# Token-major residual, output, feed-forward and down projections, and norms taken one 128-token tile at a time

## The chip, the core and the metric

The kernel runs on one core of one Trainium2 chip. The metric is the device time of one execution in microseconds (us), lower is better. An execution is one launch of the whole program, both layers included.

## What is computed

The program computes a decoder trunk of two layers for 256 tokens and a model width of 1024, in float32:

```python
for l in range(2):
    sh1, sc1, g1, sh2, sc2, g2 = split(silu(c) @ ada_w[l] + ada_b[l], 6)      # six vectors of 1024
    h = rmsnorm(x, norm_mix_w[l]) * (1 + sc1) + sh1
    x = x + g1 * hybrid_mixer(h, ...)      # ends in merged @ w_o
    h = rmsnorm(x, norm_ffn_w[l]) * (1 + sc2) + sh2
    ffn = swiglu(h, w1, w3, w2) if l == 0 else moe_swiglu(h, ...)   # dense 2816 wide; top 2 of 8 experts
    x = x + g2 * ffn
return rmsnorm(x, final_norm_w)
```

The mixer projects h to nine groups of 512 columns (f, q, ab, ac, ah, i, v, u, g) and to three gates of 1024. It runs a short convolution, a gated linear recurrence (nine levels of masked scores) and a spatial gating unit (from u and v, called sgu), projects each of the three results to 1024 columns, adds them under their gates to `merged` and multiplies by `w_o`.

## The kernel before

**Precision.** Every weight piece of 128 x 1024 floats is loaded by a DMA into a ring of 11 slots (`raw`) and split into a rounded high part, by ScalarE, and the low rest, by VectorE, in a ring of 6 slots (`split`). The activations are split in the same way (`hS[:, 0]` and `hS[:, 1]`). A product is three matmuls: high by high, high by low and low by high. So a piece costs one DMA, one ScalarE copy (line 1254), one VectorE subtraction (lines 1507 and 2046) and its matmuls, and all the matmuls are issued by one helper (line 671).

**Two shapes of matmul.** Feature-major (`tile`, `project`, `down`): 128 x 128 weights stand still and 256 tokens move, so a piece takes 24 matmuls of 256 columns. The result has features on the partitions. Token-major (`project_rows`, `half_rows`): 128 tokens stand still and 512 weight columns move, so a piece takes 12 matmuls of 512 columns for the two tiles of 128 tokens. In the kernel before, the groups i and v, the gates and the branch projections are token-major. The residual `xT`, `w_o` (8 pieces per layer), the dense `ffn_w1` and `ffn_w3` (44 pieces) and `ffn_w2` (22 pieces) are feature-major. The experts multiply 128 gathered rows at a time, with 6 matmuls of 512 columns per piece.

**Norms.** `norm` on ScalarE and VectorE works on all 256 tokens at once. ScalarE squares `xT`, TensorE sums the squares over the features by a matmul with ones (`stat_sum`, `stat_pair`), ScalarE takes the root, VectorE the reciprocal, then eight chunks of 128 features are scaled, shifted and split. TensorE meanwhile sums the modulation vectors over the partitions (`ada_sum`: 16 instructions of one column) and, before the feed-forward part, runs filler matmuls (`stream`, 12 instructions).

**Order.** All is written out by hand. Each engine runs its own list. `unit_plan` and `event_plan` list which PSUM banks are used in which order and who empties them; `high_parts` and `low_parts` say up to which piece ScalarE and VectorE split before their next step; `dense_pieces` gives the order in which SyncE issues the DMAs, and the next DMA into a slot waits until its piece is used up. The sums behind the modulation vectors are products on VectorE (`product`, lines 1585 and 1588), set among the pieces by lists such as `FFN_TAKE` and `DOWN_TAKE`.

**Levels of the recurrence.** `level(l, j)` on TensorE stands between projection units. VectorE prepares its operands (`prepare(l, j)`) and merges its scores from PSUM (`keep_scores(l, j)`, line 1777, and line 1773 for the last). Levels alternate between two pairs of banks, so TensorE's event n + 2 waits until event n is emptied; after level 8 comes `sgu_mix`, which uses the banks of level 7. In both layers the levels 0 to 8 follow the units ab0, ab1, ac0, ac1, ah0, ah1, i0, v0 and v1.

**From layer 1's w_o to the experts.** After `w_o` and the norm the kernel turns `xT` and the normed rows from feature-major to token-major (32 transposes, line 1068), computes router logits, picks the experts, ranks the tokens and gathers the first 128 rows (`gather`), and the first expert's matmuls begin.

Of the kernel before, what the change touches and what calls it, by code (L numbers as in the profile page):

```python
# [51 lines left out]
WO_ORDER = [(0, 0), (1, 0), (0, 1), (1, 1), (2, 0), (2, 1), (3, 0), (3, 1)]  # L52
# [25 lines left out]
ADA_ORDER = [0, 1, 2, 3, 4, 5, 6, 7, 11, 8, 9, 10]  # L78
FFN_ADA = [5, 6, 7]
DOWN_ADA = [11]  # L80
NORM_SUMS = [7, 6, 11]
LAST_ROWS = 3
BANKWISE = NF - LAST_ROWS
DOWN_TAKE = [int(f % 2 == 0 and f < 2 * KD) for f in range(NF)]
assert sum(DOWN_TAKE) == KD * len(DOWN_ADA)
FFN_TAKE = [3, 3, 2] * 3 + [0, 0]
assert sum(FFN_TAKE) == KD * len(FFN_ADA)
FFN_SUM_AT = next(p for p in range(NF // 2) if sum(FFN_TAKE[:p + 1]) >= KD) + 1

# [9 lines left out]
FILL_NORM, FILL_LOGITS = 6, 2  # L99
# [4 lines left out]
def unit_plan():  # L104

    plan = [("c", "D")] + [(("x", j), "A") for j in range(4)] + [(("vec", 0), "A")]
    for l in range(DEPTH):
        for g in HEAD_GROUPS:
# [7 lines left out]
        plan += [((l, "wo", j), "D") for j in range(4)]  # L116
        if l == 0:
            plan += [(("ffn", j), "D") for j in range(NF)] + [(("mod", s), "D") for s in NORM_SUMS]
    plan += [(("xtok", j), "A") for j in range(3)] + [("logits", "D")]
    plan += [(("htok", j), "A") for j in range(4)] + [(("xtok", 3), "A"), ("rank", "D")]  # L120
    plan += [(("g2", j), "A") for j in range(2)]
# [3 lines left out]
def event_plan():  # L125

    plan = []
    for l in range(DEPTH):
        if l == 0:
            plan += [((0, "norm1"), "A"), (("half", 0), "D"), (("half", 1), "D")]  # L130
        else:
            plan += [((1, "norm1"), "A")]
        plan += [((l, "lev", j), "D") for j in range(NLEV)]
        plan += [((l, "sgu"), "D"), ((l, "o"), "D"), ((l, "ostat"), "A")]
        plan += [(("ada", 6 * l + s), "D") for s in (2, 4)]
        plan += [((l, "norm2"), "A"), (("ada", 6 * l + 3), "D")]
        if l == 0:
            plan += [(("ada", FFN_ADA[0]), "D")]
            plan += [("down0", "D"), ("down1", "D")]
# [10 lines left out]
def unit_signals():  # L150
# [6 lines left out]
    for key, _ in UNITS:  # L157
        kind = key[1] if len(key) == 3 and isinstance(key, tuple) else key[0]
# [3 lines left out]
        elif kind in ("i", "v", "ffn", "gatea", "gateb", "gatec", "ya", "yb", "yc"):  # L162
            used += (2 if kind[0] == "y" else 4) if key[-1] % 2 == 0 else 0
            signal[key] = ("used", used, used)
        elif kind in HEAD_GROUPS or kind == "wo":
            used += (3, 1, 2, 2)[key[-1]] if kind == "wo" else 2
            signal[key] = ("used", used, used)
        else:
            direct += 1
            used += NF if key == ("mod", NORM_SUMS[0]) else 0  # L170
# [8 lines left out]
def dense_pieces():  # L179
# [22 lines left out]
    for l in range(DEPTH):  # L202
        for g in HEAD_GROUPS:
# [2073 lines left out]
```

## Time and profile before

| what | value |
|---|---|
| median of 3 runs | 1505.9 us (1505.34 to 1507.75) |
| span of the profiled execution, first to last instruction | 1505.1 us |
| matmuls (PE) busy | 1490.6 us, 8505 instructions |
| VectorE (DVE) busy | 1299.7 us |
| ScalarE (ACT) busy | 959.8 us |
| mean granted TensorE clock | 0.994 |
| moved by DMA | 470.89 MB, 313 GB/s on average |

The profiled execution has no time of its own beside its span; its span lies 0.8 us under the median of the runs. Matmuls are pipelined and the ends of matmuls are modelled, so that a busy PE isn't proof of a PE at its peak: what a matmul costs is read from the starts of two neighbouring groups in the timeline, not from the durations. A granted clock of 1.00 is 2.4 GHz and 0.50 is 1.2 GHz.

### The profile page before, as it was taken

The page shows a single profiled execution, that of the slowest core. Times are in us where ns is not written, and L with a number is a line of the kernel's source. Part 1 is how long each engine was busy: PE and PEld are TensorE (multiplying, and loading weights), DVE is VectorE, ACT ScalarE, POOL GpSimd, SP SyncE. Part 2 cuts the span into 40 slices and gives each one's busy share as a digit, 9 for nine tenths or more (in the row PEclk, how much of TensorE's full clock was granted, in tenths as well). Part 3 has the DMA queues.
Part 4 walks back from the last instruction along what each step waited for, and adds up shares of the span by engine and source line. Part 5 has one row for each costly group of instructions (what it writes and reads, how often), then busy time and mean ns, then how long its engine had stood idle before and what let it go on. Part 6 is the DMA issues. An engine that isn't in the chain of part 4 may idle for free.

```text
span 1505.1 us, 24325 instructions
## 1 busy us (share of the span) xinstructions
PE 1490.6 (99%) x8505; PEld 1311.0 (87%) x8505; DVE 1299.7 (86%) x1529; ACT 959.8 (64%) x1107; POOL 26.7 (2%) x44
## 2 busy tenths in 40 slices
PE   8999999999999999999999999999999999999997
PEld 7999888999999999888988888888888888888886
DVE  7999787777775799787799999999999999999998
ACT  3636445444544535444588888887878878788885
POOL 0000000000000000000010000000000000000100
PEclk9999999999999999999999999999999999999999
DMA  9956498388995646588399999999999999999993
GB/s 349 341 173 221 151 331 293 103 291 297 377 410 193 210 154 218 174 291 306 109 398 397 410 394 404 372 379 409 363 392 369 382 406 364 393 369 379 411 393 139
DMA packets 210458, 470.89 MB, mean 313 GB/s; under 512 B 16156, under 2 KB 93140, under 8 KB 210388
## 3 DMA queue, kind: packets, MB, share of 16 engines
q1 hardware_dynamic: 206624, 457.27, 83.0%
q0 software_dynamic: 3488, 12.59, 2.1%
q8 instruction: 44, 0.72, 0.2%
q14 instruction: 26, 0.21, 0.0%
q10 hardware_dynamic: 276, 0.09, 0.0%
HBM read 454.69 MB, written 15.21 MB: 312 GB/s over the span
## 4 chain that ended last, share of the span: by engine, by line
PE 94%; DVE 3%; DMA 1%; ACT 0%; issue 0%; DVEq 0%; SPq 0%; ACTq 0%
PE psU L671 68%; PE psA L671 24%; DVE split L2046 1%; PE psA L1155 1%; DMA raw<-in_ada_w_dram 1%; PE psU L1115 0%; DVE adacc L1655 0%; PE psU L1068 0%; PE psA L747 0%; ACT split L1254 0%; DVE adacc L1652 0%; DVE work L1655 0%; DVE merged L1677 0%; DVE xT L2027 0%; DVE work L1652 0%
## 5 line engine op out<-in xcount | busy, mean ns | idle before, releaser
L1254 ACT ACTIVATE split<-raw 128x1024 fp32r<-128x1024 f32 x750 | 781.8, 1061 | 300.0 <-PE psU L671 134.3
L2046 DVE TENSOR_TENSOR split<-raw,split 128x1024 fp32r<-128x1024 f32 x528 | 617.2, 1221 | 22.8 <-ACT split L1254 10.4
L671 PE MATMUL psU<-split,yS 128*128 128x512 f32 x2448 | 564.6, 390 | 0.1
L671 PEld LDWEIGHTS psU<-split,yS 128*128 128x128 f32 x2448 | 458.0, 188 | 94.9 <-DVE split L2046 0.8
L671 PE MATMUL psU<-hS,split 128*128 128x256 f32 x2688 | 331.0, 285 | 0.1
L1507 DVE TENSOR_TENSOR split<-raw,split 128x1024 fp32r<-128x1024 f32 x222 | 264.2, 1219 | 77.3 <-ACT split L1254 76.5
L671 PEld LDWEIGHTS psU<-hS,split 128*128 128x128 f32 x2688 | 326.3, 193 | 1.5 <-issue 1.2
L671 PE MATMUL psA<-split,hidE 128*128 128x512 f32 x1056 | 246.0, 392 | 0.0
L671 PEld LDWEIGHTS psA<-split,hidE 128*128 128x128 f32 x1056 | 196.4, 188 | 40.2
L671 PE MATMUL psU<-split,hS 128*128 128x512 f32 x720 | 168.4, 391 | 0.0
L671 PEld LDWEIGHTS psU<-split,hS 128*128 128x128 f32 x720 | 134.3, 188 | 28.0 <-DVE split L1507 0.4
L671 PE MATMUL psA<-hid_hi,split 128*128 128x256 f32 x352 | 63.5, 283 | 0.0
L1383 ACT ACTIVATE sig<-psU 128x512 f32<-128x512 f32 x24 | 13.0, 596 | 72.9 <-PE psU L671 72.9
L1588 DVE SCALAR_TENSOR_TENSOR adacc<-raw,cact,adacc 128x1024 f32<-128x1024 f32 x42 | 53.8, 1282 | 2.2 <-DMA raw<-in_ada_w_dram 0.4
L671 PEld LDWEIGHTS psA<-hid_hi,split 128*128 128x128 f32 x352 | 55.0, 192 | 0.0
L2202 DVE TENSOR_TENSOR hidE<-psA,hidE 128x512 fp32r<-128x512 f32 (+1 forms) x48 | 29.5, 643 | 14.4 <-ACT hidE L1254 14.4
L1254 ACT ACTIVATE hidE<-psA 128x512 fp32r<-128x512 f32 (+1 forms) x48 | 25.2, 561 | 18.1 <-PE psA L1155 18.1
L671 PE MATMUL psA<-hid,split 128*128 128x256 f32 x128 | 36.2, 283 | 0.0
L2195 DVE TENSOR_TENSOR sig<-sig,psU 128x512 f32<-128x512 f32 (+1 forms) x48 | 29.3, 639 | 6.6 <-PE psU L671 6.6
L1254 ACT ACTIVATE work<-psU 128x512 f32<-128x512 f32 x26 | 14.5, 600 | 21.7 <-PE psU L671 21.2
L1448 ACT ACTIVATE sig<-psU 128x512 f32<-128x512 f32 (+1 forms) x48 | 25.3, 562 | 4.2 <-PE psU L671 4.2
L1155 PEld LDWEIGHTS psA<-ident,sig 128*128 128x128 f32 x176 | 21.2, 141 | 4.2
(267 smaller groups left out, 824.5 us busy)
## 6 DMA issues: line engine op xcount, KB each, us to landing
raw<-in_moe_w_dram SPq DMA_DIRECT2D x496, 512.0 KB, 5.8
raw<-in_w_in_dram SPq DMA_DIRECT2D x116, 512.0 KB, 6.0
raw<-in_ada_w_dram SPq DMA_DIRECT2D x96, 512.0 KB, 7.8
raw<-in_ffn_w_dram SPq DMA_DIRECT2D x66, 512.0 KB, 8.6
raw<-in_moe_w_dram SPq DMA_DIRECT2D x64, 256.0 KB, 6.2
raw<-in_w_o_dram SPq DMA_DIRECT2D x16, 512.0 KB, 5.5
token_rows<-sc SPq DMA_DIRECT2D x11, 512.0 KB, 13.0
raw<-in_w_br_a_dram SPq DMA_DIRECT2D x8, 512.0 KB, 6.6
```

Of the source, the lines that this page charges most:

```text
L671: return pe.matmul(o, a, b, start=start, stop=stop, skip_group_check=True)
L1155: last = pe.transpose(T_BANKS[g % 2][:, m * CAP:(m + 1) * CAP], sig[0:CAP, 2 + g % 2, m * P:(m + 1) * P], ident[0:CAP, 0:CAP])
L1254: return act.activation(o, i, ACT.Copy)
L1383: act.activation(sig[:, j, :], bank[:, :], ACT.Sigmoid).then_inc(s_uA, 1)
L1448: act.activation(sig[0:CAP, g % 2, 0:width], psU[3 if g == MIXED else g % 2][0:CAP, 0:width], ACT.Silu).then_inc(s_silu, 1)
L1507: TTN(split[:, n % SPL, 1, :], raw[:, SPLIT_POS[n] % RAW, :], split[:, n % SPL, 0, :].bitcast(F32), ALU.subtract).then_inc(s_lo, 1)
L1588: STT(acc, raw[:, pos % RAW, :], cact[:, k:k + 1], acc, ALU.mult, ALU.add).then_inc(s_afree, 1)
L2046: TTN(split[:, slot, 1, :], raw[:, (RAW0 + n) % RAW, :], split[:, slot, 0, :].bitcast(F32), ALU.subtract).then_inc(s_lo, 1)
L2195: TTN(sig[0:CAP, 2 + g % 2, 0:width], s, three, ALU.mult).then_inc(s_hrow, 1)
L2202: TTN(h_lo, T_BANKS[g % 2][:, 0:len(tiles) * CAP], h_hi.bitcast(F32), ALU.subtract).then_inc(s_hlo, 1)
```

## The change

- `w_o`, `ffn_w1`, `ffn_w3` and `ffn_w2` become token-major (`rows_piece`, `down`). The last, half-wide group of the feed-forward part (2 of 22 tiles, 4 pieces) moves 256 columns per matmul as before.
- The residual is kept as rows (`xs`). `add_rows` multiplies a 128 x 512 bank by a gate row and adds it. The gate rows are broadcast: `row_sum` (two float32 matmuls of 512 columns, recorded as four instructions) takes the place of `ada_sum` for the sections 2, 5, 8, 9 and 10, and bias rows are loaded by five new DMAs on the GpSimd queue.
- The product of the feed-forward part is turned to feature-major by 44 transposes (`turn_hidden`).
- Before each of the three inner norms the last four weight pieces are held: tile 0 of the tokens runs through all four, then tile 1. The norm of a tile is a row sum on ScalarE, a root, and a scaling; `turn_tile` turns it (8 transposes), ScalarE shifts and rounds it, VectorE takes the low part. The next four pieces are held too (`rows_by_tiles`).
- In layer 1 the group v comes first, and the levels 7 and 8 follow i1 and u0. `attend` of layer 1 moves behind u1.
- For the router the rows are scaled and shifted before the turn; the expert rows need no turn. `stream` before the feed-forward part is gone. `ada_sum` or `row_sum` of most sections moves ahead of the norms.

```diff
-WO_ORDER = [(0, 0), (1, 0), (0, 1), (1, 1), (2, 0), (2, 1), (3, 0), (3, 1)]
+HEADS = [HEAD_GROUPS, ["v"] + [g for g in HEAD_GROUPS if g != "v"]]
+LEVELS = [[(g, j) for g in HEAD_GROUPS for j in range(2) if (g, j) not in NO_LEVEL][:9],
+          [(g, j) for g in ("ab", "ac", "ah", "i") for j in range(2)] + [("u", 0)]]
+ATTEND = [("u", 0), ("u", 1)]
+WO_PIECES = [(hh, q) for qs in ((0, 1), (2, 3)) for hh in range(2) for q in qs]
+HELD = 4
...
+ROW_SUMS = [2, 5, 8, 9, 10]
+DOWN_SUM_AT = {2: 7, 3: 6, BANKWISE - 1: 11}
...
+            def rows_piece(banks, q, w, tt, cols=512):
+                each = PIECE // cols
+                for kk in range(each):
+                    k = each * q + kk
+                    for wp, hp in ((0, 0), (1, 0), (0, 1)):
+                        last = mm(banks[tt][:, 0:cols], hS[:, hp, k, tt * P:(tt + 1) * P], w[wp][:, kk * cols:(kk + 1) * cols],
+                                  k == 0 and (wp, hp) == (0, 0), k == KD - 1 and hp == 1)
+                return last
+            def rows_by_tiles(n, banks):
+                ws = []
+                for q in range(4):
+                    ws.append(next_split())
+                    if q == 3:
+                        turn_tile(n, 1)
+                    pe.wait_ge(s_tl, 8 * n + q + 1)
+                    rows_piece(banks, q, ws[q], 0)
+                for q in range(4):
+                    pe.wait_ge(s_tl, 8 * n + 4 + q + 1)
+                    rows_piece(banks, q, ws[q], 1).then_inc(s_used, 1)
...
+                section_sum(6 * l + 4)
+                for hh, q in WO_PIECES[HELD:]:
+                    pe.wait_ge(s_ml, 4 * l + q + 1)
+                    ws.append(next_split())
+                    last = rows_piece(wo[hh], q, ws[-1], 0)
+                    if q == 3:
+                        last.then_inc(s_unit, 1)
+                for n, (hh, q) in enumerate(WO_PIECES[HELD:]):
+                    rows_piece(wo[hh], q, ws[n], 1).then_inc(s_used, 1)
+                    if n == 2:
+                        turn_tile(2 * l, 0)
...
+            def tile_high(n, tt):
...
                 for k in range(KD):
...
+                    ins = act.activation(xn[tt][:, k * P:(k + 1) * P], banks[k // 4][:, (k % 4) * P:(k % 4 + 1) * P],
+                                         ACT.Identity, scale=wm[:, l, second, k:k + 1], bias=mod[:, l, sh:sh + 1])
...
+                    if k % 2:
+                        copy(hS[:, 0, k - 1:k + 1, tt * P:(tt + 1) * P],
+                             xn[tt][:, (k - 1) * P:(k + 1) * P].rearrange("p (a b) -> p a b", a=2)).then_inc(s_th, 1)
...
+                ins = TTN(spare_rows(n, tt, hh), bank[:, :], row[:, o], ALU.mult)
...
+                TTN(xs[:, tt, o], xs[:, tt, o], spare_rows(n, tt, hh), ALU.add).then_inc(s_xu, 1)
...
+            def norm_tiles(n, held, row):
+                low_parts(held + 6)
+                add_rows(n, 0, 0, row)
+                add_rows(n, 0, 1, row)
+                tile_base(n, 0)
+                tile_rows(n, 0)
+                add_rows(n, 1, 0, row)
+                low_parts(held + 7)
+                tile_low(n, 0, range(2))
+                add_rows(n, 1, 1, row)
+                tile_low(n, 0, range(2, 4))
+                tile_base(n, 1)
+                tile_rows(n, 1)
+                low_parts(held + 8)
+                tile_low(n, 1, range(4))
...
                 for j in range(2):
-                    bank = unit((l, "v", j))
...
+                    if l == 0:
+                        value_rows(l, j)
+                    elif j:
+                        lows_beside((l, "u", 0))
                     keep_scores(l, 7 + j)
...
             for ch in range(KD):
                 ins = TS(g2col[:, ch * P:(ch + 1) * P], ones[:, :], mod[:, 1, 40 + ch:41 + ch], None, ALU.mult)
             ins.then_inc(s_gw, 1)
+            modulate_row(10, scale_row, 6, norm_row)
+            item_low(0, 0)
+            item_low(0, 1)
...
+            add_rows(2, 0, 0, g1row)
+            scaled_rows(0, 0)
+            add_rows(2, 0, 1, g1row)
+            scaled_rows(0, 1)
+            tile_base(2, 0)
+            router_rows(0)
+            add_rows(2, 1, 0, g1row)
+            scaled_rows(1, 0)
+            add_rows(2, 1, 1, g1row)
+            tile_base(2, 1)
+            scaled_rows(1, 1)
+            router_rows(1)
```

## Rows read from the trace of the kernel before

**Rows 1.** The page: the chain that ended last, by engine.
```profile
PE 94%; DVE 3%; DMA 1%; ACT 0%; issue 0%; DVEq 0%; SPq 0%; ACTq 0%
```

**Rows 2.** Timeline of PE in layer 1: start, us, operation; gates and a two-matmul float32 sum.
```profile
596.22 1.88 PE L671 MATMUL psA<-work,ones 128*128 128x512 f32 x4
597.53 6.31 PE L671 MATMUL psU<-hS,split 128*128 128x256 f32 x48
...
654.51 11.04 PE L671 MATMUL psU<-split,hS 128*128 128x512 f32 x48
665.39 5.60 PE L671 MATMUL psU<-split,yS 128*128 128x512 f32 x24
```

**Rows 3.** Timeline: ACT's splits in the down projection; PE at the first turn.
```profile
464.28 1.06 ACT L1254 ACTIVATE split<-raw 128x1024 fp32r<-128x1024 f32 x1 [1.82 <-PE psA L671]
...
467.16 1.06 ACT L1254 ACTIVATE split<-raw 128x1024 fp32r<-128x1024 f32 x1 [1.82 <-PE psA L671]
...
242.56 1.04 PE L747 MATMUL psA<-ident,merged 128*128 128x128 f32 x8
243.36 5.73 PE L671 MATMUL psU<-split,yS 128*128 128x512 f32 x24
```

**Rows 4.** Timeline of PE between layer 0's w_o and the feed-forward part.
```profile
272.82 0.59 PE L671 MATMUL psA<-sig,ones 128*128 128x256 f32 x2
273.25 1.84 PE L671 MATMUL psA<-ones,work 128*128 128x1 f32 x16
274.96 1.11 PE L671 MATMUL psA<-sig,ones 128*128 128x256 f32 x4
...
283.38 28.82 PE L671 MATMUL psU<-hS,split 128*128 128x256 f32 x237
```

**Rows 5.** Timeline of PE between the down projection and layer 1's level 0.
```profile
475.79 0.92 PE L671 MATMUL psU<-ones,merged 128*128 128x1 f32 x7
...
484.29 30.80 PE L671 MATMUL psU<-hS,split 128*128 128x256 f32 x240
514.92 1.95 PE L671 MATMUL psA<-work 128*128 128x128 f32 x16
```

**Rows 6.** Groups by line, with mean ns: VectorE's split and bank times row, ScalarE's square.
```profile
L2046 DVE TENSOR_TENSOR split<-raw,split 128x1024 fp32r<-128x1024 f32 x528 | 617.2, 1221 | 22.8 <-ACT split L1254 10.4
...
L1960 DVE TENSOR_TENSOR sig<-sig,psU 128x512 f32<-128x512 f32 x16 | 10.9, 684 | 6.0 <-PE psU L671 6.0
...
L1308 ACT ACTIVATE sig<-xT 128x512 f32<-128x512 f32 x12 | 7.6, 632 | 25.0 <-DVE xT L1976 18.0 <-DVE xT L2027 7.0
```

**Rows 7.** Windows: PE, PEld, DVE, ACT, POOL busy (x), PEclk, DMA share, GB/s.
```profile
480.00:500.00 20.00, 20.00 (x144) 20.00 (x144) 19.65 (x34) 13.50 (x20) 0.00 (x0) 0.83 0.45 145
...
732.00:734.00 2.00, 2.00 (x20) 2.00 (x20) 1.87 (x3) 0.01 (x1) 0.51 (x1) 1.00 0.00 0
```

**Rows 8.** Timeline of DVE, then PE, in layer 1's levels 6 to 8.
```profile
568.34 0.69 DVE L1735 TENSOR_TENSOR work<-work 128x512 f32<-128x512 f32 x1 [0.51 <-PE psA L671]
...
569.55 1.66 DVE L1851 SCALAR_TENSOR_TENSOR work<-work,vecs 128x254 f32<-128x254 f32 x4
571.24 1.23 DVE L1864 TENSOR_TENSOR work<-work 128x1024 f32<-128x1024 f32 x1
...
577.79 0.75 DVE L1777 COPY_PREDICATED sc<-masks,psA 128x512 f32<-128x512 uint8 x1
...
561.78 5.63 PE L671 MATMUL psU<-split,hS 128*128 128x512 f32 x24
```

**Rows 9.** Timeline from layer 1's w_o to the first expert.
```profile
704.36 4.47 PE L671 MATMUL psU<-hS,split 128*128 128x256 f32 x36
...
735.38 3.78 PE L671 MATMUL psU<-rtw,merged 128*128 128x64 f32 x32
...
737.08 1.65 DVE L2050 TENSOR_SCALAR work<-ones,mod 128x128 f32<-128x128 f32 x8
...
746.86 25.30 PE L671 MATMUL psU<-split,yS 128*128 128x512 f32 x110
```

More of the change, by code:

```diff
@@ L765, in ada_sum, with turn_merged @@
-            def ada_sum(s, bank=None, ks=range(KD)):
+            def turn_merged(l, pair):
+                banks = open_event((l, "merge", pair))
+                for i in (2 * pair, 2 * pair + 1):
+                    pe.wait_ge(s_mg, 8 * l + 4 + 2 * pair + 2)
+                    for m in range(2):
+                        col = (2 * i + m) % 4 * P
+                        for tt in range(TT):
+                            row = merged[:, 4 * pair + 2 * tt:4 * pair + 2 * tt + 2, :].rearrange("p a b -> p (a b)")
+                            last = pe.transpose(banks[i % 2][:, m * T + tt * P:m * T + (tt + 1) * P], row[:, col:col + P],
+                                                ident[:, :])
+                    last.then_inc(s_ev if i % 2 else s_mt, 1)
@@ L776, in fill, with section_sum @@
+            def section_sum(s):
+                row_sum(s) if s in ROW_SUMS else ada_sum(s)
             def fill(bank, count):
@@ L1024, in dense_ffn @@
-                scale = open_unit(("mod", NORM_SUMS[0]))
-                ada_sum(NORM_SUMS[0], scale, range(5))
-                stat_sum(stat, 1).then_inc(s_used, 1)
-                stat_pair(stat, 3, 3)
-                ada_sum(NORM_SUMS[0], scale, range(5, KD))
-                for s in NORM_SUMS[1:]:
-                    ada_sum(s)
+                    for tt in range(TT):
+                        for hh in HALVES:
+                            last = down(f, w, tt, hh)
+                    last.then_inc(s_used, 1)
@@ new lines, in dense_ffn @@
+                    if f == 0:
+                        turn_hidden(len(GROUPS) - 1)
+                    elif f == 1:
+                        row_sum(5)
+                    elif f in DOWN_SUM_AT:
+                        ada_sum(DOWN_SUM_AT[f])
+                pe.wait_ge(s_flo, TT * len(GROUPS))
+                ws = []
+                for tt in range(TT):
+                    for hh in HALVES:
+                        for f in range(BANKWISE, NF):
+                            if (tt, hh) == (0, 0):
+                                ws.append(next_split())
+                            last = down(f, ws[f - BANKWISE], tt, hh)
+                            if (tt, hh) == (1, 1):
+                                last.then_inc(s_used, 1)
+                                if f == NF - 2:
+                                    turn_tile(1, 0)
+                        if (tt, hh) != (1, 1):
+                            last.then_inc(s_dn if (tt, hh) == (0, 0) else s_ev, 1)
@@ L1262, in _ @@
             for j in range(4):
-                copy(xT[:, 2 * j:2 * j + 2, :].rearrange("p a b -> p (a b)"), unit(("x", j))[:, :]).then_inc(s_uA, 1)
+                copy(sig[:, j, :], unit(("x", j))[:, :]).then_inc(s_uA, 1)
             copy(vecs[:, :], unit(("vec", 0))[:, 0:NA_ROWS + NB_ROWS]).then_inc(s_uA, 1)
@@ L1984, in mixer @@
[L1984 to L2006 removed]
+                        modulate_row(6 * l + 2, g1row, 6 if l else 1)
```

807 lines of the change are left out of this document (450 added, 357 removed).

## The prediction

> **What bounds the kernel now.** I read the page first: the chain that ended last is 94% TensorE (PE) [rows 1]. Busy shares can't say whether PE runs at its peak, because the ends of matmuls are modelled. So I went on to the timeline of PE, and took the time between the starts of neighbouring groups. Two things are to be seen there. In steady stretches PE has no gap, and its pace differs by shape [rows 2, 3]. And there are three places, at the three inner norms, where the main matmuls stop for 8 to 19 us (the first two are [rows 4, 5]). The change works on both. The kernel stays bound by PE, so each part is priced as what it adds to or takes from PE's list, or as a wait that PE newly has.
>
> **Part 1, the shape.** 48 matmuls of 512 columns take 665.39 - 654.51 = 10.88 us, 0.2267 us each [rows 2]; a piece of 12 takes 2.72 us. In the down projection ScalarE's splits, which wait for a slot that PE gives back, come 467.16 - 464.28 = 2.88 us apart [rows 3]: 24 matmuls of 256 columns, 0.120 us each. The change turns 2 x 8 pieces of w_o, 40 of ffn_w1 and ffn_w3 (4 of the 44 stay at 256 columns) and 22 of ffn_w2: 78 pieces x (2.88 - 2.72) = 12.5 us less. Both ends of each difference are read to 0.01 us, so 11.5 to 13.5.
>
> The row shows that halving the number of matmuls gives 0.0135 us per pair. The Trainium skill, page TensorE: Matmul & The Clock Gate, section Back-to-back issue gap, gives a gap of the columns over 2.4 GHz plus 2.5 ns, by which a pair of 256 columns would cost 218.3 ns and one of 512 columns 215.8 ns. By that rule 936 pairs would save 2.3 us only. The trace doesn't agree with its absolute figures (226.7 ns measured for 512 columns), and I take the trace.
>
> **Part 2, turning the hidden rows.** 44 transposes. Eight take 243.36 - 242.56 = 0.80 us [rows 3], so 4.4 us more. Their ScalarE copies and VectorE subtractions lie beside the next pieces: per group of 8 pieces VectorE has 8 splits at 1.22, 5 modulation products of the same size (estimate 1.3) and four operations of 0.68 [rows 6], some 19 us against PE's 8 x 2.72 + 0.8 = 22.6 us. Cover 3.6 us; if it were gone, PE would lose the excess six times. I take 0.
>
> **Part 3, sums.** `ada_sum` takes 274.96 - 273.25 = 1.71 us [rows 4], a `row_sum` 597.53 - 596.22 = 1.31 us [rows 2]. For the sections 2, 5 and 8: 3 x 0.4 = 1.2 us less. The bias rows come by GpSimd's queue, long before they are used; 0.
>
> **Part 4, the norm before the feed-forward part.** From the last w_o matmul to the first of ffn_w1 pass 283.38 - 272.82 = 10.56 us [rows 4]. Afterwards PE has here, or nearby, the same two sums (3.4 us), 16 transposes (1.6 us) and waits. For the waits I follow tile 0, t = 0 at its last w_o matmul. VectorE multiplies and adds a half in 2 x 0.72, the square takes 0.63 [rows 6], and root, reciprocal and the scaling are small operations of 0.2 to 0.4 (estimates from the same rows): the rows are ready at about 3.6. PE has three pieces of tile 1 until 4.1, so no wait. It turns until 4.9 and has one more piece until 6.2. ScalarE needs about 1.05 us per pair of chunks, VectorE has a split of 1.2 us queued ahead of the first low part: first pair ready at 6.9, wait 0.65. Tile 1's squares stand on ScalarE behind all four pairs of tile 0, so its turn comes 0.4 late. Waits 1.1 us. Sum 6.1, so 4.4 us less. Bounds: waits of 0 and of 3.5 (each pair at double cost).
>
> **Part 5, the norm before layer 1.** Before: from 475.79 to 484.29 are 8.5 us, and the ten pieces up to level 0 take 514.92 - 484.29 = 30.6 instead of 10 x 2.88, 1.8 us lost [rows 5]: the granted clock is 0.83 on average over those 20 us, so 20 x 0.17 / 0.5 = 6.8 us at 1.2 GHz [rows 7]. Together 10.3. After: three sums 5.1, turns 1.6, waits 1.1: 7.8. So 2.4 us less, with the same bounds.
>
> **Part 6, v first.** The group v moves whole, so its PE time is equal, but the levels lose two units of cover. Before, PE had level 7 after v0 and level 8 after v1. Now level 7 comes after i1, at 561.8 on the old clock [rows 8], level 8 one unit later (5.8 + 0.8) at 568.4, and `sgu_mix` right behind at 569.2. VectorE is busy without a break there. It can do the operands of level 8 at 567.8, since its 0.51 us of idle [rows 8] goes: level 8 may start at 569.1. Then in its list stand the last tap (1.66), the product (1.2), and only then `keep_scores(7)` (two of 0.7): 573.3 [rows 8]. `sgu_mix` needs these banks, and everything on PE is queued behind it: u1, `attend`, g. PE waits 0.3 + 0.4 + 3.5 = 4.2 us. Bounds: 0 (if VectorE ran ahead by the modulation products that come earlier) and 6.
>
> **Part 7, from w_o to the experts.** Before: 746.86 - 704.36 = 42.5 us from the first w_o matmul to the first expert's [rows 9]. After, with w_o's start at 704.4: four pieces and a turn to 716.0, `row_sum(10)` to 717.3, tile 0 to 722.8. VectorE has in its list, ahead of the first `add_rows`: the splits of the held pieces until 718.7, the `g2col` columns 1.65 [rows 9], `modulate_row(10)` 2.6 and two expert splits 2.3, so it begins at 725.3, 2.5 us late. A tile costs 4 x 0.72 + 2 x 0.61 = 4.1, then 0.8 of square, 0.6 of root and reciprocal, 1.4 of scaling and shift. Tile 0 is ready at 731.6 while PE wanted it at 726.9; PE's last w_o piece ends at 733.4; tile 1 is ready at 737.9. Then half a turn 0.4, copy 0.6, half the logits of a tile 0.9 (32 take 3.5 [rows 9]), VectorE's choice 1.6, rank and its use 2.0, first half of the gather with splits 3.6: 747.3. Add section 9's sum, now earlier, 1.3: 748.6. That is 1.7 us later than 746.9, though w_o itself is 8 x 0.16 = 1.3 shorter, already counted: 3.0 us more. The five DMAs added on GpSimd's queue are issued a stage earlier, ahead of its wait for section 9's event; they hold nothing up. Bounds: -2 (VectorE in time) and +7.
>
> **The clock.** Around the norm before layer 1 it fell to 1.2 GHz after a stretch of one-column sums [rows 5, 7]; at the router, with like sums and transposes behind them, it stayed at 2.4 GHz [rows 7]. The first place gets shorter. The new idle at the router (4 us, twice) may bring a fall. Bounds 0 and 5.5 us; 1.5, near the lower end because the row nearest to it shows 1.00.
>
> **Sum.** -12.5 + 4.4 - 1.2 - 4.4 - 2.4 + 4.2 + 3.0 + 1.5 = -7.4 us on a profiled 1505.1; the median of the runs lies 0.8 above the span. 1505.9 - 7.4 = 1498.5 us. A measurement of this kernel tells 0.2% (3 us) from no change.
>
> **Rivals.**
> - *The new waits are covered* (VectorE is early enough at `sgu_mix` and at the router, no fall of the clock): -12.5 + 4.4 - 1.2 - 4.4 - 2.4 = -16.1, 1489.8 us. For it: VectorE had some idle, 0.51 us before level 8's operands. Against it: that is all it had in the 30 us ahead of level 8. Chance 0.15.
> - *Tile chains are longer than priced*: each norm waits at the upper bound (2.4 us more, twice) and the router 2 more: +6.8, 1505.3 us. For it: eight ScalarE steps that each wait for the one before, a form with no row here. Chance 0.17.
> - *The clock decides, slower*: each low-activity place (the two norms, `sgu_mix`, the router) gets a fall of 6.8 us, as long as the one around 485 [rows 7]. Each costs 3.4, together 13.6, in place of the 1.5: 1510.6 us. It decides from 24 us of half clock in all. For it: every such place has idle that the old one hadn't. Against it: they are shorter. Chance 0.08.
> - *A pair saves 2.5 ns, slower*: if the 512-column pace of w_o and the feed-forward part were near that of two of 256 (2.3 us saved in place of 12.5), the time is 1508.7 us. Against it: the gates show the pace over hundreds of matmuls [rows 2]. Chance 0.05. It is the rule of the page named in part 1.
> - *It doesn't do what it says*: VectorE can't follow in the feed-forward part, so that PE keeps 2.88 per piece: 40 x 0.16 = 6.4 us back, 1504.9 us. Chance 0.03.
>
> **The numbers.** My forecast has 0.52, with its own range from 1493 to 1502. Down to the first rival and up over the second, the range 1490 to 1504 leaves out about 0.2. Faster by over 0.2% (under 1502.9): 0.49 of the forecast, the first rival, and 0.10 of the second and the last: 0.74. Within 0.2%: 0.13. Slower: 0.13.
>
> **What would show it.** In the changed kernel: ScalarE's splits 2.72 us apart in the down projection; transposes of `sig` 0.4 us per four; from the last w_o matmul of tile 0 to the first of ffn_w1 some 7 us; PE idle of 3 to 4 us before `sgu_mix` with VectorE named as its releaser; PE idle of about 4 us before `turn_tile` at the router. The forecast is wrong if PE doesn't wait at `sgu_mix`, if the piece stays at 2.88, or if the clock is at 0.50 for more than 10 us.

## The result, and the profile after

The changed kernel takes 1515.9 us (median of 4 runs, 1515.7 to 1516.2) against 1505.6 for the kernel before, timed beside it: a ratio of 1.0056 with a 95% interval of 1.0043 to 1.0068. The medians are 10.3 us apart; the ratio, on which the rest of this text leans, makes it 8.4 us (6.5 to 10.2). Forecast was 1498.5, a gain of 7.4. The profiled executions say the same: a span of 1513.9 us after, 1505.1 before, 8.8 us more.

**The shape did what it should.** The timeline of TensorE (PE) in the feed-forward part (start, us, operation), and of ScalarE (ACT) in the down projection:

```profile
307.55 22.03 PE L731 MATMUL psU<-split,hS 128*128 128x512 f32 x96
329.42 1.04 PE L1068 MATMUL psA<-ident,sig 128*128 128x128 f32 x8
330.21 22.03 PE L731 MATMUL psU<-split,hS 128*128 128x512 f32 x96
```
```profile
432.30 1.06 ACT L1339 ACTIVATE split<-raw 128x1024 fp32r<-128x1024 f32 x1 [1.66 <-PE psA L731]
435.02 1.06 ACT L1339 ACTIVATE split<-raw 128x1024 fp32r<-128x1024 f32 x1 [1.66 <-PE psA L731]
```

Eight pieces take 329.42 - 307.55 = 21.87 us, 2.73 each, and the splits come 2.72 us apart, where they came 2.88 apart [rows 3]. Turning the hidden rows costs 330.21 - 329.42 = 0.79 us per eight from start to start, and the first matmul behind each group of turns takes 0.09 us more than the others. PE does not wait for VectorE (DVE) there.

**The time went into waits.** The list of PE's waits between 240 and 760 us (in total, times, longest), its first lines; before, this stretch had one wait of 0.6 us:

```profile
PE psA L799 <- DVE split L1656: 5.1, 2, 2.5
PE psA L799 <- DVE work L2278: 3.1, 1, 3.1
...
```

Four of them are 2.5 to 3.1 us long: at the turn of tile 1 in each of the two norms, ahead of `sgu_mix`, and at the router's first turn. PE's timeline shows them in place. First the norm before the feed-forward part (it answers to [rows 4]), then the norm before layer 1 ([rows 5]), then levels 7, 8 and `sgu_mix` ([rows 8]), then the router up to the first expert ([rows 9]):

```profile
274.99 1.63 PE L731 MATMUL psU<-split,hS 128*128 128x512 f32 x6
276.92 4.58 PE L731 MATMUL psU<-split,hS 128*128 128x512 f32 x18 [0.30 <-DVE hS L1839]
284.05 1.97 PE L799 MATMUL psA<-ident,merged 128*128 128x128 f32 x8 [2.54 <-DVE split L1656]
...
306.76 1.03 PE L1068 MATMUL psA<-ident,sig 128*128 128x128 f32 x8
...
476.74 4.58 PE L731 MATMUL psU<-split,hS 128*128 128x512 f32 x18 [0.98 <-DVE hS L1839]
483.86 1.09 PE L799 MATMUL psA<-ident,merged 128*128 128x128 f32 x8 [2.55 <-DVE split L1656]
...
493.23 7.00 PE L731 MATMUL psU<-hS,split 128*128 128x256 f32 x57
...
576.17 1.16 PE L731 MATMUL psA<-work 128*128 128x128 f32 x8 [0.26 <-DVE work L1955]
580.32 3.60 PE L731 MATMUL psA<-wT,merged 128*128 128x128 f32 x16 [3.00 <-DVE sc L1996]
583.58 6.15 PE L731 MATMUL psU<-hS,split 128*128 128x256 f32 x48
...
734.40 1.94 PE L799 MATMUL psA<-ident,work 128*128 128x128 f32 x8 [3.05 <-DVE work L2278]
...
742.51 1.04 PE L799 MATMUL psA<-ident,work 128*128 128x128 f32 x8
...
747.44 0.36 PE L731 MATMUL psU<-route,tri 128*128 128x8 f32 x2 [1.64 <-DVE route L2317]
...
749.85 6.07 PE L731 MATMUL psA<-sc,work 128*128 128x128 f32 x32 [0.85 <-DVE sc L2326]
755.68 1.63 PE L731 MATMUL psU<-split,yS 128*128 128x512 f32 x6
```

**And into the clock.** Windows of 4 us, four of the changed kernel and then two of the kernel before. Each row has the length, the busy time of PE, weight loads, DVE, ACT and GpSimd (with the number of instructions), then the granted clock, the DMA share and GB/s:

```profile
284.00:288.00 4.00, 3.95 (x16) 3.56 (x17) 0.43 (x2) 2.59 (x7) 0.00 (x0) 0.63 0.45 131
...
580.00:584.00 4.00, 3.68 (x18) 3.71 (x19) 3.02 (x4) 0.58 (x1) 0.00 (x0) 0.57 0.00 0
...
748.00:752.00 4.00, 3.15 (x15) 3.05 (x16) 2.26 (x16) 0.00 (x0) 0.00 (x0) 0.50 0.01 4
752.00:756.00 4.00, 4.00 (x26) 3.96 (x26) 0.69 (x1) 1.58 (x3) 0.00 (x0) 0.68 0.00 0
```
```profile
276.00:280.00 4.00, 4.00 (x21) 3.73 (x20) 3.10 (x6) 2.16 (x4) 0.00 (x0) 0.58 0.05 17
280.00:284.00 4.00, 4.00 (x14) 3.26 (x13) 4.00 (x12) 2.60 (x6) 0.00 (x0) 0.56 0.00 0
```

At each of the four waits the granted clock falls to 1.2 GHz for some 3.4 us, and for 6.8 at the waits for the ranks and the selection. (A window at 0.57 holds 4 x 0.43 / 0.5 = 3.4 us at the lower level. The window from 484 has 0.61, those from 732 and 736 have 0.76 and 0.81.) Added up over the windows to 1500 us these are 20.6 us, against 13.8 in two falls before.

**Where the two traces part**, in us between the starts of the same groups of PE:

| stage | before | after | forecast |
|---|---|---|---|
| start to layer 0's w_o | 248.9 | 250.7 | 250.2 |
| to the first matmul of the down projection | 163.3 | 156.3 | 151.8 |
| to layer 1's level 0 (v included after the change) | 102.7 | 115.0 | 109.4 |
| to layer 1's w_o (v included before) | 189.4 | 185.8 | 183.6 |
| to the first expert | 42.5 | 47.9 | 42.9 |
| experts to the end | 758.2 | 758.2 | 758.2 |

The forecast of a stage is the time before with the terms of parts 1 to 7 that fall into it; the 1.5 us for the clock are not in the column. The four stages in the middle each come out 2 to 6 us longer than forecast.

### The profile page after: what moved, and what is told of

Same layout as the page of the kernel before. It is cut to its first block and busy times, and to the rows that moved or that the text cites. A ratio compares the mean times of both kernels' runs of the same rounds, so it can differ in the third digit from the quotient of the medians.

```text
span 1513.9 us, 22427 instructions
## 1 busy us (share of the span) xinstructions
PE 1484.2 (98%) x7543; PEld 1260.1 (83%) x7543; DVE 1300.1 (86%) x1508; ACT 961.2 (63%) x1120; POOL 30.0 (2%) x50
## 5 line engine op out<-in xcount | busy, mean ns | idle before, releaser
L731 PE MATMUL psU<-split,hS 128*128 128x512 f32 (+1 forms) x1488 | 340.7, 387 | 1.4 <-DVE hS L1839 1.3
L731 PEld LDWEIGHTS psU<-split,hS 128*128 128x128 f32 x1488 | 273.4, 190 | 58.8 <-issue 5.1
L731 PE MATMUL psU<-hS,split 128*128 128x256 f32 x1248 | 155.2, 285 | 0.1
L731 PEld LDWEIGHTS psU<-hS,split 128*128 128x128 f32 x1248 | 151.3, 192 | 1.3 <-issue 1.2
L731 PE MATMUL psA<-split,hid_hi 128*128 128x512 f32 x176 | 55.2, 395 | 0.0
L731 PEld LDWEIGHTS psA<-split,hid_hi 128*128 128x128 f32 x176 | 32.6, 188 | 6.9 <-issue 0.5
L1339 ACT ACTIVATE work<-psU 128x512 f32<-128x512 f32 x18 | 10.4, 598 | 25.4 <-PE psU L731 20.6
L731 PE MATMUL psA<-split,hid 128*128 128x512 f32 x64 | 25.0, 390 | 0.0
```

The costliest lines, as they stand in the source:

```text
L731: return pe.matmul(o, a, b, start=start, stop=stop, skip_group_check=True)
L1339: return act.activation(o, i, ACT.Copy)
```

## The experiments

The kernel before was timed beside every kernel; its median was 1507.1, 1506.2, 1507.0 and 1507.5 us on the four occasions, so a gain is read from ratios: the difference to 1.0056, times 1506 us. Spans are of one profiled execution each, with 1513.9 of the changed kernel beside them. A span has in it which falls of the clock that one execution happened to have, so spans, and sums of them, are good to a few us only; rows of equal stretches are better.

**1. Levels 7 and 8 kept early.** VectorE, layer 1:

```diff
                 lows_beside((l, "i", 1))
+                if l:
+                    keep_scores(l, 7)
                 tap(2)
                 settle()
                 TTN(AH, AH, AB, ALU.mult).then_inc(s_y, 1)
 ...
-                    elif j:
-                        lows_beside((l, "u", 0))
-                    keep_scores(l, 7 + j)
+                        keep_scores(l, 7 + j)
+                if l:
+                    keep_scores(l, 8)
```

> Edit: in layer 1 VectorE keeps the scores of levels 7 and 8 ahead of the last tap and the product of branch a's short convolution, and ahead of the piece for u; nothing else moves. Theory (four waits of about 3 us, each followed by 3.4 us at the half clock of which 1.7 is lost): the 3.00 us wait of TensorE before the mix of the gating unit (580.32 in the changed kernel) goes, the granted clock of 580 to 584 stays at full, and the median falls by 4 to 4.7 us from 1515.9, to 1511.2 to 1511.9. Rival (VectorE is what bounds this stretch whatever its order): the wait comes back at level 8, at the mix or at the attention matmuls, and the time falls by under 1 us.

Measured: ratio 1.0031 (1.0020 to 1.0041), 3.8 us better, just under the 4 to 4.7 of the theory; span 1507.3, 6.6 less. PE's timeline of this kernel, at the levels and at the norm before layer 1:

```profile
576.64 2.02 PE L731 MATMUL psA<-wT,merged 128*128 128x128 f32 x16 [0.16 <-DVE sc L1996]
578.42 5.99 PE L731 MATMUL psU<-hS,split 128*128 128x256 f32 x48
...
483.89 1.09 PE L799 MATMUL psA<-ident,merged 128*128 128x128 f32 x8 [2.54 <-DVE split L1656]
...
492.30 3.95 PE L731 MATMUL psU<-hS,split 128*128 128x256 f32 x31
```

Of the 3.00 us wait 0.16 is left and nothing else takes its place; the 16 mixing matmuls take 578.42 - 576.64 = 1.78 us at full clock, not 583.58 - 580.32 = 3.26. With the wait that makes some 4.5 us by the rows, as the theory had it. The rest of the span's 6.6 is chance: in this execution the clock did not fall behind the turns at 483.9 and at the router, though the waits ahead of them were as long as before (2.54 and 3.05 us). From the turn to the first f matmul are 8.41 us here, 9.37 with a fall.

**2. The router reordered.** VectorE: the eight `g2col` steps moved behind `router_rows(0)`, `item_low(0, 0)` and `item_low(0, 1)` into its idle times.

```diff
-            for ch in range(KD):
-                ins = TS(g2col[:, ch * P:(ch + 1) * P], ones[:, :], mod[:, 1, 40 + ch:41 + ch], None, ALU.mult)
-            ins.then_inc(s_gw, 1)
             modulate_row(10, scale_row, 6, norm_row)
-            item_low(0, 0)
-            item_low(0, 1)
```

> Edit: on VectorE the eight g2 columns (1.65 us) go behind the router rows of tile 0, and the low parts of the first two expert pieces (2.36 us) go into the idle times ahead of the second logits and ahead of the ranks; before, all 4.0 us stood ahead of the residual add of tile 0. Theory: tile 0's rows are ready about 3.3 us earlier, the 3.05 us wait of TensorE at 734.40 goes, and the clock does not fall there (1.7 us): the first expert matmul comes 4 to 5 us earlier and the median is 1511 to 1512. Rival (the chain logits, top two, ranks, gather is what counts and tile 1 is bound by its own w_o matmuls): the wait moves to tile 1's turn, and the time falls by 1.5 us at most.

Measured: ratio 1.0035 (1.0023 to 1.0047), 3.2 us better; span 1510.2, 3.7 less.

```profile
731.33 1.07 PE L799 MATMUL psA<-ident,work 128*128 128x128 f32 x8
...
738.85 1.23 PE L799 MATMUL psA<-ident,work 128*128 128x128 f32 x8 [0.50 <-DVE work L2273]
...
743.80 0.36 PE L731 MATMUL psU<-route,tri 128*128 128x8 f32 x2 [1.64 <-DVE route L2317]
...
745.63 6.63 PE L731 MATMUL psA<-sc,work 128*128 128x128 f32 x32 [0.79 <-DVE sc L2327]
752.01 8.31 PE L731 MATMUL psU<-split,yS 128*128 128x512 f32 x35
```

The turn comes 3.1 us earlier and without a wait, and the clock doesn't fall there; 0.50 us of the wait comes back at tile 1's turn. The clock still falls behind the 1.64 us, and the gather of 32 matmuls takes 6.4 us. The first expert's matmul comes 755.68 - 752.01 = 3.7 us earlier, where the theory had 4 to 5: right in mechanism, a little short in size. The interval just overlaps that of the changed kernel, so the rows carry the verdict.

**3. The fourth held piece split early**, in both norms (ScalarE, then VectorE):

```diff
-                high_parts(held + 7)
+                high_parts(held + 8)
                 tile_high(n, 0)
 ...
-                tile_low(n, 0, range(2, 4))
+                tile_low(n, 0, [2])
+                low_parts(held + 8)
                 tile_base(n, 1)
+                tile_low(n, 0, [3])
                 tile_rows(n, 1)
-                low_parts(held + 8)
```

> Edit: in both norms done by tiles, the high and low part of the fourth held piece are made during tile 0's step, where ScalarE and VectorE are idle, and no longer between tile 1's normed rows and TensorE's turn of them. Theory: TensorE's waits of 2.54 and 2.55 us at the turns of tile 1 shorten by 1.2 to 1.6 us each, -2.4 to -3.2 us in all; if the shorter wait also keeps the clock at full, another 1.7 us each: 1509.5 to 1513.5, by the clock. Rival (tile 1's rows are late by ScalarE's squares and root anyway and the piece was hidden): under 0.5 us each, 1515 to 1516.

Measured: ratio 1.0029 (1.0017 to 1.0041), 4.1 us better; span 1509.8, 4.1 less.

```profile
282.87 1.06 PE L799 MATMUL psA<-ident,merged 128*128 128x128 f32 x8 [1.09 <-DVE merged L1831]
...
285.53 19.56 PE L731 MATMUL psU<-split,hS 128*128 128x512 f32 x84 [0.20 <-DVE hS L1838]
304.93 1.06 PE L1068 MATMUL psA<-ident,sig 128*128 128x128 f32 x8
```

The wait falls from 2.54 to 1.09 us, with the releaser now the normed rows (`merged`), and the clock stays at full in both norms. From the turn to the first turn of hidden rows 304.93 - 282.87 = 22.06 us pass, against 306.76 - 284.05 = 22.71: the fall had cost 0.65 us here, not the 1.7 of the theory. At full clock PE has to wait 0.20 us for the low parts of tile 1 behind the turn (at 285.53): ScalarE's pace sets that start, and at half clock PE is merely less early for it.

**4. Fillers in the waits**, to measure the clock by itself: 12 calls of `stream` ahead of the turns, then 6.

```diff
-                    ws.append(next_split())
                     if q == 3:
-                        turn_tile(n, 1)
+                        turned = open_event(("xt", n, 1))
+                        stream(turned[0], 12)
+                    ws.append(next_split())
+                    if q == 3:
+                        turn_tile(n, 1, turned)
```

> Edit: 12 matmuls of 256 columns whose result is not used (0.24 us each, 2.8 us) stand on TensorE in three of the waits: ahead of tile 1's turn in both norms and ahead of tile 0's turn in the router; every wait is otherwise as in the changed kernel. It measures the clock by itself. Theory: the waits stay as long, but the granted clock no longer falls after them (3.4 us at half each, 1.7 us lost): 3 x 1.7 = 5.1 us less, 1510.8, or somewhat more where a filler delays a turn by some tenths. Rival (the fall costs nothing since what follows waits for other engines): 1516 to 1517.

Measured: ratio 1.0088 (1.0074 to 1.0101), 4.8 us worse; span 1518.1.

```profile
281.74 5.34 PE L731 MATMUL psA<-sgub,ones 128*128 128x256 f32 x24
286.92 1.04 PE L801 MATMUL psA<-ident,merged 128*128 128x128 f32 x8
```

I had sized it wrongly. A float32 matmul is two instructions (x24 for 12), so a filler took 0.43 us and the twelve 5.2 us, in a wait of 3.0. It cost what it was too long (5.2 - 3.0 = 2.2 us, three times) and only part of it came back from the clock. With 6:

> Edit: the changed kernel with 6 filler matmuls (12 instructions of 0.22 us, 2.7 us) in the three waits of about 3 us, where the run with 12 had fillers of 5.3 us, longer than the waits, and paid 2.3 us at each. Theory: nothing is late now and the clock stays at full behind each: by the stages of the run with 12, the work behind the two turns took 0.7 to 0.9 us less at full clock than at half, since ScalarE's steps bound it part of the way, and the router 1.7: 2.3 to 5.1 us less than the changed kernel, 1511 to 1513.5. Rival (the clock costs nothing): 1516.

Measured: ratio 1.0043 (1.0029 to 1.0057), 2.0 us better, and 3.8 by the span (1510.1); the intervals of the two ratios overlap, so this gain is shown by rows more than by medians.

```profile
281.69 2.75 PE L731 MATMUL psA<-sgub,ones 128*128 128x256 f32 x12
284.39 1.09 PE L801 MATMUL psA<-ident,merged 128*128 128x128 f32 x8
...
306.52 1.03 PE L1073 MATMUL psA<-ident,sig 128*128 128x128 f32 x8
```

From turn to turn 22.13 us, as in experiment 3. The rival "the clock costs nothing" falls by these rows, and so does a price of 1.7 us for the fall at this place.

**5. Tile 1's squares ahead of tile 0's last pair**, on top of experiment 3. ScalarE:

```diff
                     if k == 4:
                         act.wait_ge(s_ev, at + 1)
+                    if k == 6 and between:
+                        between()
 ...
-                tile_high(n, 0)
-                tile_square(n, 1, 0)
-                tile_square(n, 1, 1)
-                tile_root(n, 1)
+                def next_root():
+                    tile_square(n, 1, 0)
+                    tile_square(n, 1, 1)
+                    tile_root(n, 1)
+                tile_high(n, 0, next_root)
```

> Edit: as the run with the fourth held piece early, and ScalarE also squares tile 1's rows and takes their root ahead of the last two chunks of tile 0, not behind them. Theory: in the run before this TensorE still waited 1.09 and 1.10 us at the turns of tile 1, for rows that stood behind ScalarE's four pairs of chunks (1.29 us a pair); one pair less ahead of them takes these waits away: 2 x 1.1 = 2.2 us less than that run, about 1509, with its clock unchanged at full. Rival (the last pair of tile 0 is then late for TensorE in its place, or the low parts are): the same wait behind the turn, 1511 to 1512.

Measured: ratio 1.0057 (1.0044 to 1.0071), all of experiment 3's gain lost. VectorE's timeline shows why:

```profile
282.89 0.43 DVE L1842 TENSOR_TENSOR hS<-merged,hS 128x256 fp32r<-128x256 f32 x1 [1.71 <-ACT hS L1339]
283.23 0.15 DVE L1827 RECIPROCAL nst<-nst 128x1 f32<-128x1 f32 x1
```

I moved ScalarE's step and left VectorE's order. The last low part of tile 0 (L1842) now waits 1.71 us for a pair that ScalarE does later, and the reciprocal of tile 1 is queued behind it. Two engines that hand work to each other must be reordered together. Mended (the piece's low part behind the first low part, the last one behind `tile_rows(n, 1)`):

```diff
-                tile_low(n, 0, range(2))
+                tile_low(n, 0, [0])
+                low_parts(held + 8)
+                tile_low(n, 0, [1])
                 add_rows(n, 1, 1, row)
                 tile_low(n, 0, [2])
-                low_parts(held + 8)
                 tile_base(n, 1)
-                tile_low(n, 0, [3])
                 tile_rows(n, 1)
+                tile_low(n, 0, [3])
```

> Edit: as the run with the squares of tile 1 early, but VectorE makes the last low part of tile 0 behind tile 1's normed rows (in that run it stood ahead of them and waited for ScalarE's last pair, so the rows came at 283.2, later than before), and the low part of the held piece goes into its idle time behind the first low part. Theory: the rows of tile 1 are ready 1 us or more earlier than in the run with the held piece alone, TensorE's waits of 1.09 and 1.10 us at the two turns fall under 0.3, and a wait of up to 0.5 us stands at tile 0's last chunks: spans 1 to 2 us under that run's 1509.8. Rival (ScalarE's step of 1.29 us a pair bounds the whole norm, in whatever order): under 0.5 us, with the wait moved behind the turn.

Measured: ratio 1.0019 (1.0010 to 1.0027), 5.6 us better than the changed kernel; span 1508.3. The profile names no wait of PE at either turn of tile 1. By the starts 0.5 us is still lost there: 277.51 plus 18 x 0.227 is 281.6, and the turn starts at 282.12. In the changed kernel it was 3.05:

```profile
282.12 1.06 PE L799 MATMUL psA<-ident,merged 128*128 128x128 f32 x8
...
474.37 4.76 PE L731 MATMUL psU<-split,hS 128*128 128x512 f32 x18 [1.06 <-DVE hS L1842]
478.97 1.06 PE L799 MATMUL psA<-ident,merged 128*128 128x128 f32 x8
```

**6. The three together** (experiments 1, 2 and the unmended 5):

> Edit: the changed kernel with the three reorderings together: levels 7 and 8 kept early, the router's g2 columns and expert pieces later, the held piece and the squares of tile 1 early. Theory: the three act at different places and add up: by the spans, 6.6 (levels), 3.7 (router) and 4.1 plus 2.2 (norms), of which some 1.5 of the first is scatter: about 15 us less than the changed kernel, 1499 to 1501, which is 5 to 6 us under the kernel before. Rival (the gains overlap, as a shared DMA stream or a later wait takes part back): over 1504.

Measured: ratio 1.0000 (0.9991 to 1.0009), span 1504.1. Expected were 1499 to 1501, from a sum of spans into which I had put 2.2 us for the squares. Experiment 5 doesn't give that gain; it takes some back. The two waits ahead of tile 1's turns are 2.32 us each where experiment 3 has 1.09 and 1.10 (2.5 us), and the fall of the clock at the first of them is back (0.65). With the 2.2 that is the whole shortfall. Of the two waits, of 2.32 us each, the one at 283.6 was followed by a fall and the one at 483.4 was not.

**7. And with work in the wait for the ranks.** On PE the turn of the g2 columns goes behind `logits(1)`, then one `stream`; `FILL_LOGITS` is 6.

> Edit: the same three, and at the router TensorE turns the g2 columns behind the second logits, with one filler matmul, in the time in which it waits for the ranks; the filler ahead of tile 1's turn is 6 in place of 4. Theory: in the run with the router reordered the clock still fell to half from 745 to 751.5 us behind a wait of 1.64 us and one of 0.79 us, and the 32 gather matmuls took 6.6 us in place of 3.8; with work in the wait the fall goes, and another 3 us with it: 1496 to 1498. Rival (a fall comes all the same, by the short matmuls of the ranks): the time of the run with three reorderings, within 1 us.

Measured: ratio 0.9987 (0.9977 to 0.9998), span 1501.8, 2.3 less than without, where 1496 to 1498 was expected, 3 us under that sum. The interval overlaps that of experiment 6, so the rows carry the reading.

```profile
738.20 0.39 PE L731 MATMUL psU<-route,tri 128*128 128x8 f32 x2 [0.24 <-DVE route L2324]
...
740.06 3.84 PE L731 MATMUL psA<-sc,work 128*128 128x128 f32 x32 [0.80 <-DVE sc L2334]
743.67 6.71 PE L731 MATMUL psU<-split,yS 128*128 128x512 f32 x28
```

The wait of 1.64 us is 0.24, the one of 0.80 stays, the clock stays at 1.00, and the gather takes 3.61 us. The short matmuls are the same as before, so the fall came with the wait for the ranks; the three later kernels with this edit (experiment 8 and its two steps) have no fall there either.

**8. All of it, with the squares mended.**

> Edit: the version with the router's g2 turns behind the second logits, levels early and held pieces early, with the squares in the order of the run before this one. Theory: its two waits of 2.3 us become under 0.5: 1.8 us twice, and 1.7 or less for the one fall of the clock that was left (284 to 288): 3.6 to 5.3 us under its span of 1501.8, so 1496.5 to 1498.2, and a median of about 1499. Rival (what TensorE waits for in the norms is ScalarE's chain as a whole): 1501 to 1502.

Measured: ratio 0.9950 (0.9937 to 0.9963), 1499.7 us against 1507.0, span 1496.5. It beats the kernel before by 0.5%, 7.5 us. In its profiled execution the clock is never below full up to the experts, and that is about half of the gain: at the same mean granted clock of 0.998, one of its executions has a span of 1498.5 us and two of the kernel before have 1502.1 and 1502.2. Two single steps on top of it:

> Edit: as the run before this one, with the turn of tile 0 one piece earlier on TensorE (behind two and not three of the four held pieces of tile 1) in the norm before the feed-forward part and in the one before layer 1. It asks what the waits of 0.30 and 1.06 us at tile 0's first chunks are made of. Theory: the normed rows of tile 0 are there by then (in the run with the held piece alone at 471.4, and the turn began at 472.3), so these waits shrink by up to 0.3 and 0.6 us: 0.5 to 0.9 us less. Rival: the rows are not there yet and TensorE stops ahead of a turn instead: 0 to 1 us more.

Measured: ratio 0.9957 (0.9943 to 0.9971), the same within the intervals. PE waited 0.69 us ahead of the earlier turn for the rows (L1836) in the first norm, and saved its 0.30 behind it. In the second the wait went from 1.06 to 1.04: ScalarE was still busy with the two splits of held pieces (470.34 to 472.25, then the first pair of tile 0), so an earlier turn gained nothing.

> Edit: the version with all reorderings (the one of the squares in the mended order), and of ScalarE's two scale-and-shift steps per pair of chunks the first no longer signals and is waited for; the second still is, ahead of the copy that reads both. It asks what the 1.29 us per pair, for which the prediction took 1.05, are made of. Theory (each wait for the step just issued costs about 0.15 us beyond the work): the two steps take 0.95 us with two such waits, some 0.75 to 0.8 with one, so a pair comes to 1.1 us, TensorE's waits of 0.30 and 1.06 us at tile 0's first chunks shrink by 0.1 to 0.2 each, and the time falls by 0.5 us at most, not to be told apart by the medians, only in the rows. Rival (the step is its fixed cost and the wait is free): 0.93 to 0.95 us for two as before.

Measured: ratio 0.9941 (0.9928 to 0.9953), span 1496.6, so no difference that can be told. Its edit is `else: link(ins)` to `elif k % 2: link(ins)` in `tile_high`. ScalarE's timeline, of experiment 8 and then of this kernel:

```profile
276.38 0.93 ACT L1413 ACTIVATE merged<-psA,mod,wm 128x128 f32<-128x128 f32 x2
...
277.67 0.94 ACT L1413 ACTIVATE merged<-psA,mod,wm 128x128 f32<-128x128 f32 x2
```

```profile
277.39 0.79 ACT L1413 ACTIVATE merged<-psA,mod,wm 128x128 f32<-128x128 f32 x2
...
278.54 0.79 ACT L1413 ACTIVATE merged<-psA,mod,wm 128x128 f32<-128x128 f32 x2
```

Two steps take 0.79 us where they took 0.93 to 0.95, and a pair 278.54 - 277.39 = 1.15 where it took 1.29. So one wait for the step just issued costs 0.14 us.

## Why the prediction was wrong, step by step

- **Part 1, shape: right.** 2.72 to 2.73 us per piece, where 2.72 was taken. The rule of the Trainium skill (page TensorE: Matmul & The Clock Gate, section Back-to-back issue gap) would have left 2.3 us of the 12.5, and makes a piece 12 x 0.2158 = 2.59 us (an estimate by it); the piece's 2.73 us disagree, as the rows before did.
- **Part 2: right.** Turns take 0.79 per eight, covered on VectorE and ScalarE. The 0.09 us behind each group of them were not priced, 0.5 in all.
- **Part 3, sums: a term mis-sized.** A `row_sum` was priced at 1.31 us from its start to the next group's, and by that measure it takes 1.32 (719.91 to 721.23). But the first matmul behind it starts a group that is 0.4 us too long, in the changed kernel and in the kernel before alike (there the first matmul at 597.53 takes 0.52 us, the others 0.12). The changed kernel's timeline, from the middle of a `row_sum` on:

```profile
683.40 1.88 PE L731 MATMUL psA<-adacc,ones 128*128 128x512 f32 x4
684.72 6.05 PE L731 MATMUL psU<-split,yS 128*128 128x512 f32 x24
690.60 9.68 PE L731 MATMUL psU<-split,hS 128*128 128x512 f32 x42
```

  The 24 matmuls take 690.60 - 684.72 = 5.88 us, not 24 x 0.2267 = 5.44: the first takes 0.63. So a `row_sum` costs 1.7 us; an `ada_sum` costs 1.8, with 0.1 behind it in the same way. The saving is 0.1 us each and not 0.4, and each of the five new ones comes some 0.4 dearer than the 1.3 that it was priced at, 2.0 in all.
- **Parts 4 and 5, the norms: the first failed step, "Waits 1.1 us" each.** Between starts, PE loses 0.57 us ahead of the group at 276.92 (274.99 plus 6 x 0.227 is 276.35) and 3.05 at 284.05 (276.92 plus 18 x 0.227 is 281.00), 3.6 together; in the second norm 1.24 and 3.04, 4.3. Both lie just beyond the upper bound of 3.5. Two things were missed. "ScalarE needs about 1.05 us per pair" is 1.29, for each of its steps waits for the one before (one such wait costs 0.14, by the last experiment): four pairs put tile 1's squares 1 us later. And the prediction has one split queued ahead of tile 0's first low part but not the one of the piece after it, which VectorE makes behind tile 1's rows and for which PE waits before it turns them. The releaser named is that `split`; experiment 3 takes 1.45 us off at one stroke, and experiment 5, mended, all but 0.5 of the rest.
- **Part 6, v first: right in mechanism and nearly in size.** 4.2 us of waits were priced, 0.3 + 3.2 came (level 8 starts at 576.17, the eight matmuls of a level take 0.91, and `sgu_mix` starts at 580.32). Experiment 1 removes the 3.2, by moving `keep_scores` ahead of the two steps that the prediction named and of a split; the 0.3 ahead of level 8 stays (0.26).
- **Part 7, the router: right to the first turn, short after it.** Tile 0's turn was put 27.2 us behind w_o's start and came 734.40 - 707.82 = 26.6 behind; tile 1's was put at 33.5 and came at 34.7. From there 9.4 us were given to logits, choice, ranks and gather, and 13.2 were taken: 2.2 of the difference are the gather at half clock (5.83 against 3.61 in experiment 7), 0.55 the ranks at half clock, the rest halves of a turn and of the logits that were whole ones.
- **The clock: the second failed step, 1.5 us.** Row 732:734 at 1.00, on which the low value leant, has PE busy for all of its 2.00 us; the change brought idle to that place. Equal stretches with and without a fall give its price: 0.7 at the first norm (22.71 against 22.06), 1.0 at the second (9.37 against 8.41), 1.5 at `sgu_mix`, 1.3 between the router's turns (8.11 against 6.79 in experiment 1), 2.8 at ranks and gather: 7.2 us in place of 1.5. "If the clock is at 0.50 for more than 10 us" was named as what would prove the forecast wrong; it was 20.6. As a sign that was weak: the kernel before has 13.8.
- **The sum.** 8.8 - (-7.4) = 16.2 us were missed: 2.5 and 3.2 in the waits of the norms, 5.7 in the clock, 0.9 at the router, -0.7 at `sgu_mix`. That makes 11.6. Of the other 4.6 us about 2.5 can be named: 1.6 are four of the five row sums (the fifth lies at the router and is in its 0.9), 0.5 the matmuls behind the turns of the hidden rows, and 0.4 the third and fourth piece of layer 0's `w_o`, whose 24 matmuls take 5.86 us, not 5.44. (In layer 1 they do too, again within the router's 0.9.) The last 2.1 us are spread in tenths and were not tried. None of these 4.6 us was tested by a run of its own.
- **The rivals.** Nearest came *the clock decides, slower* (1510.6): its four places are the right four. That its time is near as well is in part luck: it has 13.6 us for the clock where 7.2 are found (falls of 3.4 us, not 6.8, at three of the four places, each at less than half its length), and lacks 5.7 us of norm waits, which was the rival *tile chains are longer than priced*. Each was written as if the other didn't hold, but one wait makes both: the idle and, behind it, the fall. Their joint case stood nowhere, and it happened.

So the forecast's idea, that token-major shapes pay 12 us on PE, was right. What gave it back were the waits left by the order of small steps on the two helpers, the falls of the clock at them, and terms priced too low. Experiment 8 comes out at the forecast time (0.9950 x 1505.6 = 1498), but that is not the forecast's sum come true: the row sums are as dear in it, and its clock is fuller than was forecast.

## What to carry to other kernels

A norm that is done tile by tile hides nothing by itself. Write the lists of VectorE and ScalarE in order with start times, and for each wait of TensorE ask which step stands ahead of its releaser that nobody needs yet; here moving such steps gained 3 to 4 us each time, and making one of them faster (the last experiment) nothing that could be told. Reorder both sides of a handshake together. Price a new wait of TensorE like those here with a fall of the clock on top, as one case and not as two. And read the price of a small group of matmuls up to the second matmul behind it, not to the first.

## What the runs showed of the hardware

- With TensorE's main work stopped for 2.3 to 3.1 us the granted clock fell to 1.2 GHz in some profiled executions and not in others, at the same place with the same wait (a fall at 485 in the changed kernel, none in experiment 1). A wait of 1.64 and one of 0.8 us, with eight short matmuls between, had a fall at or right behind them in all nine profiled executions that have both (6.8 us in seven, 3.4 in two), and none in the four in which work was put into the first. Waits of 1.1 us alone had none.
- A fall cost between a fifth and nearly half of its length: 0.65 us of 3.4 where ScalarE was the pace, 1.5 of 3.4 where PE was. The timed executions of the kernel before say the same: 12 with a mean granted clock of 0.997 or 0.998 have a span of 1502.6 us on average, 4 with 0.992 or 0.993 have 1508.5. That is 5.9 us for some 14 us more at 1.2 GHz (estimate, 0.0047 x 1506 / 0.5), 0.42 of the length. The Trainium skill, page TensorE: Matmul & The Clock Gate, section Terms, puts the penalty at the throttled time x (1 - K/N), half of it; the rows make that an upper bound, 10.3 us here for 20.6, where 7.2 are found.
- The first matmul behind a two-matmul float32 sum of 512 columns takes 0.4 us more than those after it, at all seven such sums of the changed kernel: 0.63 us instead of 0.23 with 512 columns, 0.52 instead of 0.12 with 256. Behind eight transposes it takes 0.09 more.
- ScalarE's scale-and-shift of 128 x 128 takes 0.47 us when it is waited for at once and 0.14 less when it is not.
